# Two norms at a block boundary merged, and the first norm's sums moved into the time of the modulation weights

## The reference, cut to what matters

```
def rmsnorm(x, g):
    return x * rsqrt(mean(x*x) + 1e-6) * g

# first block, layer l
mod = cond @ ada_w[l] + ada_b[l];  sh1, sc1, g1, sh2, sc2, g2 = split(mod, 6)
h = rmsnorm(x, norm1_g[l]) * (1 + sc1) + sh1
x = x + g1 * mixer(h);  x = x + g2 * swiglu(rmsnorm(x, norm2_g[l]) * (1 + sc2) + sh2)
...
x = rmsnorm(x, final_g)                       # end of the first block
# second block, layer 0
h  = rmsnorm(x,   g_mix[0]) * (1 + ca)   + sa
hc = rmsnorm(ctx, g_mix[0]) * (1 + ca_c) + sa_c
q, k, v, u = split(h @ w_in[0]) ...
```

## Time and profile before

| | |
|---|---|
| time, median of 3 runs | 3628.51 us (3627.23 to 3632.27) |
| time of the profiled execution | 3632.27 us |
| span of the profiled execution, first to last instruction | 3631.0 us |
| PE busy | 3426.8 us (94%) |
| POOL, DVE, ACT busy | 1579.2, 1337.1, 794.5 us |
| mean DMA rate | 96 GB/s |
| mean granted TensorE clock | 0.980 |

### The profile page before, as it was taken

How to read it: one execution, slowest core, us unless ns; L and a number is a source line. 1 busy time by engine, 2 the same in 40 slices (tenths; PEclk the granted TensorE clock), 3 DMA queues, 4 the chain that set the end, 5 groups by cost and what they waited for, 6 DMA issues and landing times.

```text
span 3631.0 us, 42550 instructions
## 1 busy us (share of the span) xinstructions
PE 3426.8 (94%) x17456; PEld 2690.6 (74%) x17456; DVE 1337.1 (37%) x2287; ACT 794.5 (22%) x1603; POOL 1579.2 (43%) x996
## 2 busy tenths in 40 slices
PE   5999999999999999999999699889999989889998
PEld 3767777788876677777778577778888878667886
DVE  5853313311158433132111665651211255551113
ACT  2234411100022444111000334320100123420111
POOL 2423266566644133664665331234333333235664
PEclk9999999999999999999999899999999999999999
DMA  6344123333233341335443211122433311114221
GB/s 204 109 134 139 46 81 107 112 95 93 81 99 122 121 136 47 93 99 161 126 140 91 71 36 36 35 80 75 149 109 107 108 53 58 35 47 137 95 93 58
DMA packets 403370, 346.80 MB, mean 96 GB/s; under 512 B 9701, under 2 KB 400613, under 8 KB 403178
## 3 DMA queue, kind: packets, MB, share of 16 engines
q1 hardware_dynamic: 395328, 336.62, 29.7%
q10 hardware_dynamic: 7850, 7.47, 0.7%
HBM read 341.96 MB, written 2.10 MB: 95 GB/s over the span
## 4 chain that ended last, share of the span: by engine, by line
PE 88%; DVE 6%; ACT 3%; DMA 1%; issue 1%; POOL 1%; ACTq 0%; DVEq 0%; SPq 0%; POOLq 0%
PE psum L571 25%; PE psum L572 24%; PE psum L573 24%; PE psum L553 2%; PE psum L812 2%; PE psum L927 1%; PE psum L956 1%; DVE psum L1782 1%; PE psum L800 1%; PE psum L744 1%; PE psum L640 1%; PE psum L787 1%; DVE k L2261 1%; DMA raw_weights<-in_ada_w 1%; PE psum L785 1%
## 5 line engine op out<-in xcount | busy, mean ns | idle before, releaser
L513 POOL TENSOR_SCALAR weights_hi<-raw_weights 128x1024 fp32r<-128x1024 f32 (+3 forms) x496 | 500.3, 1009 | 1980.9 <-PE psum L573 1667.0
L571 PE MATMUL psum<-h_hi,weights_hi 128*128 128x512 f32 (+1 forms) x2832 | 1143.4, 404 | 69.6 <-DVE h_lo L1806 51.4
L516 POOL TENSOR_TENSOR weights_lo<-raw_weights,weights_hi 128x1024 fp32r<-128x1024 f32 (+3 forms) x496 | 1088.0, 2194 | 41.4
L572 PE MATMUL psum<-h_lo,weights_hi 128*128 128x512 f32 (+1 forms) x2832 | 1077.8, 381 | 0.0
L573 PE MATMUL psum<-h_hi,weights_lo 128*128 128x512 f32 (+1 forms) x2832 | 1077.0, 380 | 0.0
L571 PEld LDWEIGHTS psum<-h_hi,weights_hi 128*128 128x128 f32 x2832 | 540.5, 191 | 229.9 <-issue 108.7
L572 PEld LDWEIGHTS psum<-h_lo,weights_hi 128*128 128x128 f32 x2832 | 541.2, 191 | 115.7 <-issue 15.9
L573 PEld LDWEIGHTS psum<-h_hi,weights_lo 128*128 128x128 f32 x2832 | 539.1, 190 | 110.5
L571 PE MATMUL psum<-hidden_hi,weights_hi 128*128 128x512 f32 (+1 forms) x1120 | 413.8, 369 | 0.0
L572 PE MATMUL psum<-hidden_lo,weights_hi 128*128 128x512 f32 (+1 forms) x1120 | 413.7, 369 | 0.0
L573 PE MATMUL psum<-hidden_hi,weights_lo 128*128 128x512 f32 (+1 forms) x1120 | 413.1, 369 | 0.0
(11 more groups left out here) (264 smaller groups left out, 3616.3 us busy)
## 6 DMA issues: line engine op xcount, KB each, us to landing
raw_weights<-in_ada_w SPq DMA_DIRECT2D x96, 1024.0 KB, 5.3
raw_weights<-in_w_mlp SPq DMA_DIRECT2D x64, 1024.0 KB, 5.2
raw_weights<-in_w_in SPq DMA_DIRECT2D x54, 1024.0 KB, 5.4
raw_weights<-in_w_ffn_in SPq DMA_DIRECT2D x88, 512.0 KB, 5.2
raw_weights<-in_w_out SPq DMA_DIRECT2D x16, 1024.0 KB, 4.9
raw_weights<-in_w_ffn_out SPq DMA_DIRECT2D x16, 1024.0 KB, 5.0
raw_weights<-in_w_in SPq DMA_DIRECT2D x30, 512.0 KB, 4.6
raw_weights<-in_w_branch SPq DMA_DIRECT2D x56, 128.0 KB, 2.2
```

The source lines that it names most:

```text
L513: gpsimd.tensor_scalar(whi[:, r, c0:c1], raw[:, raw_slot, c0:c1], 1.0, 1.0, ALU.mult, ALU.mult).then_inc(*split_hi.up(*key, half))
L516: gpsimd.tensor_tensor(wlo[:, r, c0:c1], raw[:, raw_slot, c0:c1], whi[:, r, c0:c1].bitcast(F32), ALU.subtract).then_inc(*split.up(*key, half))
L571: tensor.matmul(out, sh, mh, start=first, stop=False, skip_group_check=shared)
L572: tensor.matmul(out, sh, ml, start=False, stop=False, skip_group_check=shared)
```

## The change

Two places are rewritten.

**Start.** The raw buffers are no longer zeroed and SP issues its first three slabs at once. ACT issues the layer's columns ahead of x, then does the sines, the squares of x and the root, and only then the copy of the "start" row. DVE does the sines' product, query bias, the additions of squares and the reciprocal before ada_finish("start"). PE makes the sums of norm1 after seven of the eight slabs of "start". The group "norm1" of layer 0 is empty: its two slabs go to the end of "rope", in the order behind the slab of B's values.

**Boundary.** final1 and in1 are merged for the 512 tokens. Behind each residual slice ACT makes two squares, of x and of x * final_g, and DVE two additions. PE sums both. ACT and DVE compute the joint factor through logarithms: log1 = Ln(mean1 + eps), inverse1 = Exp(-log1), mean2 * inverse1 on DVE, Ln(... + eps), + log1 on DVE, Exp(-0.5 ...). The column of the scale takes final_g in (scales_g1). X itself is scaled behind in1, by leave(), with Exp(-0.5 log1). The context's squares, sum, root and reciprocal, the lambdas and the columns of in1 move into the last feed-forward of the first block; the context's two matmuls stand between its last up projection and its last down projection. norm_g1, lambda_columns and layer_columns_2 get places of their own in SBUF for that.

```diff
-        g["norm1", l] = slots(l, 8, 10)
-        g["rope", l] = slots(l, 10, 14)
+        g["norm1", l] = slots(l, 8, 10 if l else 8)
+        g["rope", l] = slots(l, 10 if l else 8, 14)
...
         part("B", "v", 0)
+        ada_some("rope", 4, 6)
...
+    gf1 = top.take("norm_g1", [P, KT])
+    lams = top.take("lambda_columns", [P, 8])
+    pcol2 = top.take("layer_columns_2", [P, 2 * KT + 4 + 1])
...
-    work2 = Map(nc, ffn2.at).take("squares_2", [P, 3, TA])
+    sums2 = Map(nc, ffn2.at)
+    work2 = sums2.take("squares_2", [P, 3, TA])
+    roots = sums2.take("roots", [P, 2, T])
+    log1, inverse1 = roots[:, 0, :], roots[:, 1, :]
...
-            if n < RAW:
-                sync.wait_ge(*dve_misc.at("raw", r))
-            elif order[n - RAW][0][0] == "ada":
+            if n >= RAW and order[n - RAW][0][0] == "ada":
                 sync.wait_ge(*ada_row.at(*order[n - RAW][0]))
-            else:
+            elif n >= RAW:
...
-        def norm(segs, work, which, l):
+        def sums(segs, work, which, l):
...
+        def norm(segs, work, which, l):
+            if (which, l) != ("norm1", 0):
+                sums(segs, work, which, l)
...
+        def sum_of(which, l, s, n, bk, work, x0, x1):
+            tensor.wait_ge(*free[bk])
+            tensor.wait_ge(*paired.at(which, l, s, KT - 2))
+            tensor.matmul(bank[bk][:, 0:n], meanm, part_of(work, 0, x0, x1), start=True, stop=False)
+            tensor.wait_ge(*squared.at(which, l, s, KT - 1))
+            tensor.matmul(bank[bk][:, 0:n], meanm, part_of(work, 1, x0, x1), start=False,
+                          stop=True).then_inc(*meaned.up(which, l, s))
+
+        def enter(segs):
+            sum_of("final1", None, 0, T, 2, work1, TC, TA)
+            sum_of("in1", 0, 0, T, 7, work2, TC, TA)
+            free[6] = h_lo.at("in1", 0, 1, KT - 1)
+            for k in range(KT):
+                pending[k] = [h_lo.at("in1", 0, s, k) for s in range(2)]
+            free[4], free[5] = h_lo.at("in1", 0, 0, KT - 1), h_lo.at("in1", 0, 1, KT - 1)
+            free[2], free[7] = dve_misc.at("log12"), dve_misc.at("tokens", KT - 1)
...
+                if l == DEPTH - 1 and t0 == CHUNKS1[-1][0]:
+                    sum_of("ctx1", 0, 0, TC, 6, work2, 0, TC)
...
-            norm([(TC, TA, TC, 1), (0, TC, 0, 2)], work2, "in1", L)
+            both = [(TC, TA, TC, 1), (0, TC, 0, 2)]
+            if L:
+                norm(both, work2, "in1", L)
+            else:
+                enter(both)
...
-        finish(ada_steps("start"))
+        start = ada_steps("start")
+        for _ in range(ROUND - 1):
+            next(start)
+        sums([(TC, TA, 0, 0)], work1, "norm1", 0)
+        finish(start)
         for l in range(DEPTH):
             first_layer(l)
-        norm([(TC, TA, 0, 0)], work1, "final1", None)
...
+        layer_columns(0)
         scalar.dma_start(X[:, :, TC:TA], a["x_t"].rearrange("(k p) t -> p k t", p=P)).then_inc(*loaded["x"].up())
...
+                scale = gf1[:, k:k + 1] if (which, l, s) == ("in1", 0, 0) else 1.0
                 scalar.activation(part_of(work, 1 + (k + 1) % 2 if k else 0, x0, x1), X[:, k, x0:x1],
-                                  ACT.Square).then_inc(*squared.up(which, l, s, k))
+                                  ACT.Square, scale=scale).then_inc(*squared.up(which, l, s, k))
...
+        def enter_root():
+            scalar.wait_ge(*meaned.at("final1", None, 0))
+            scalar.activation(log1, bank[2][:, :], ACT.Ln, bias=eps[:, 0:1]).then_inc(*act_misc.up("log1"))
+            scalar.wait_ge(*act_misc.at("log1"))
+            scalar.activation(inverse1, log1, ACT.Exp, scale=-1.0).then_inc(*act_misc.up("inverse1"))
+            scalar.wait_ge(*dve_misc.at("mean2"))
+            scalar.activation(bank[7][:, :], bank[7][:, :], ACT.Ln, bias=eps[:, 0:1]).then_inc(*act_misc.up("log2"))
+            scalar.wait_ge(*dve_misc.at("log12"))
+            scalar.activation(bank[7][:, :], bank[7][:, :], ACT.Exp, scale=-0.5).then_inc(*rooted.up("in1", 0, 0))
+
         def norm(segs, which, l, hi):
-            root(segs, which, l)
+            if (which, l) == ("in1", 0):
+                enter_root()
+            elif (which, l) != ("norm1", 0):
+                root(segs, which, l)
...
+                if l == DEPTH - 1 and t0 == CHUNKS1[1][0]:
+                    lambdas(0)
+                    scalar.wait_ge(*loaded["g1"].at())
+                    for n in range(KT):
+                        square(n, [(0, TC, 0, 2)], work2, "ctx1", 0, [loaded["ctx"].at()])
...
+                layer_columns2(0)
             feed(l)
+            if l == DEPTH - 1:
+                scalar.wait_ge(*meaned.at("ctx1", 0, 0))
+                scalar.activation(bank[6][:, 0:TC], bank[6][:, 0:TC], ACT.Sqrt,
+                                  bias=eps[:, 0:1]).then_inc(*rooted.up("in1", 0, 1))
...
                 square(n, seg, work1, *key, [summed.at(l, "down", CHUNKS1[-1][0], n, 0)])
-
-        def layer_columns(l):
-            scalar.dma_start(pcol[:], a["cols1"][l]).then_inc(*loaded["cols"].up(l))
+                if l == DEPTH - 1:
+                    square(n, seg, work2, "in1", 0, [summed.at(l, "down", CHUNKS1[-1][0], n, 0)])
...
+            if L == 0:
+                scalar.wait_ge(*scaled.at("in1", 0, 0, KT - 1))
+                scalar.activation(bank[7][:, :], log1, ACT.Exp, scale=-0.5).then_inc(*act_misc.up("rstd1"))
...
         scalar.wait_ge(*loaded["cond"].at())
         scalar.activation(cond_sigmoid[:], cond_in[:], ACT.Sigmoid).then_inc(*act_misc.up("cond"))
-        finish(ada_steps("start"))
         scalar.wait_ge(*dve_misc.at("angles"))
         scalar.activation(ropec[:], ropec[:], ACT.Sin)
         scalar.activation(ropes[:], ropes[:], ACT.Sin).then_inc(*act_misc.up("sines"))
-        layer_columns(0)
         for n in range(KT):
             square(n, [(TC, TA, 0, 0)], work1, "norm1", 0, [loaded["x"].at()])
+        root([(TC, TA, 0, 0)], "norm1", 0)
+        finish(ada_steps("start"))
         scalar.dma_start(gf1[:], a["final1_cols"]).then_inc(*loaded["g1"].up())
         for l in range(DEPTH):
             first_layer(l)
-        root([(TC, TA, 0, 0)], "final1", None)
-        scalar.wait_ge(*loaded["ctx"].at())
-        for n in range(KT):
-            square(n, [(TC, TA, TC, 1), (0, TC, 0, 2)], work2, "in1", 0, [summed.at("final1", n), loaded["ctx"].at()])
         for dst, name in ((cos2, "cos2"), (sin2, "sin2"), (perm2, "perm2"), (edge, "edge")):
             scalar.dma_start(dst[:], a[name]).then_inc(*loaded["axial"].up())
         scalar.dma_start(gf2[:], a["g_final_cols"]).then_inc(*loaded["g2"].up())
-        layer_columns2(0)
-        lambdas(0)
...
-        for r in range(RAW):
-            vector.memset(raw[:, r, :], 0.0).then_inc(*dve_misc.up("raw", r))
...
+        def enter():
+            vector.wait_ge(*meaned.at("in1", 0, 0))
+            vector.wait_ge(*act_misc.at("inverse1"))
+            vector.tensor_tensor(bank[7][:, :], bank[7][:, :], inverse1, ALU.mult).then_inc(*dve_misc.up("mean2"))
+            vector.wait_ge(*act_misc.at("log2"))
+            vector.tensor_tensor(bank[7][:, :], bank[7][:, :], log1, ALU.add).then_inc(*dve_misc.up("log12"))
+            vector.wait_ge(*rooted.at("in1", 0, 0))
+
+        def leave():
+            vector.wait_ge(*act_misc.at("rstd1"))
+            for k in range(KT):
+                vector.scalar_tensor_tensor(out=X[:, k, TC:TA], in0=X[:, k, TC:TA], scalar=gf1[:, k:k + 1],
+                                            in1=bank[7][:, :], op0=ALU.mult,
+                                            op1=ALU.mult).then_inc(*dve_misc.up("tokens", k))
...
-                then = None
+                    lambdas(0)
+                    second_scales(0)
+                    then = [([(0, TC, 0, 2)], work2, "ctx1", 0)]
                 if t0 == CHUNKS1[-1][0]:
-                    then = (work1, "norm1", l + 1) if l < DEPTH - 1 else (work1, "final1", None)
+                    seg = [(TC, TA, 0, 0)]
                     if l < DEPTH - 1:
+                        then = [(seg, work1, "norm1", l + 1)]
                         first_scales(l + 1)
+                    else:
+                        then = [(seg, work1, "final1", None), (seg, work2, "in1", 0)]
+                        vector.wait_ge(*rooted.at("in1", 0, 1))
+                        vector.reciprocal(bank[6][:, 0:TC], bank[6][:, 0:TC]).then_inc(*inverted.up("in1", 0, 1))
+                        vector.wait_ge(*inverted.at("in1", 0, 1))
                 residual(("down", t0), l, 5, [(TC, TA, 0, 0)], then)
...
+            if L == 0:
+                vector.wait_ge(*dve_misc.at("scales", "in1", 0, 2))
+                vector.wait_ge(*loaded["g1"].at())
+                vector.tensor_tensor(col[:, 0, :, 1], col[:, 0, :, 1], gf1[:], ALU.mult).then_inc(*dve_misc.up("scales_g1"))
...
             norm(both, "in1", L, gh, gl)
+            if L == 0:
+                leave()
...
         angles()
```

(17 more changed lines are left out.)

49 lines of the change are left out of this document (30 added, 19 removed).

## The result

| | before | after |
|---|---|---|
| time, median of 4 runs each on one chip | 3629.45 us | 3587.32 us (3585.99 to 3587.93) |
| ratio, with its 95% interval | | 0.9883 [0.9872, 0.9895] |
| span of the profiled execution | 3631.0 us | 3585.5 us |
| mean granted TensorE clock | 0.980 | 0.982 |

The change saves 42.1 us, 1.2%. The profiled executions are 45.5 apart, because the one of before, 3632.27, was above its median.

What follows compares the result with a forecast made beforehand. TensorE, busy in 94% of the span, was taken as the bound, so only its idle holes pay: 20.0 - 2.0 + 18.9 - 1.0 = 35.9 us saved, 3592.6 against the median of 3628.5, range 3584 to 3603.

Steps and rivals of the forecast that it cites:

- Start: Before the first projection matmul: it moves from 65.86 to 45.9, gaining 20.0 us, bounds 16.5 and 21.
- rival (b): At the start, three early slabs starve the small constants: start gains 14, total 30, 3598.6 us; chance 0.12.
- Two slabs in top: Two moved ada slabs now cost TensorE time in top of the first layer: 2.0 us, bounds 2 and 5.
- Boundary: Between first and second block: the hole before the second block's first matmul closes by 18.9 us, bounds 15 and 21.5.
- ACT has five transfers to issue first, so about 2.4: At the boundary, before the chain of logarithms: five transfer issues, 0.46 us apart, occupy ACT until 2025.1.
- Rival (a): At the boundary, one table set serves Ln and Exp: factor ready 2.4 us earlier, 3590; chance 0.08.
- leave(): Ahead of rope2: eight scalings, 5.36 us, and a 0.7 wait fit DVE's 6.77 idle; costs nothing, uncovered up to 6.
- the context's sums: Last feed-forward of the first block: the context's two matmuls now stand in TensorE's busy stretch, costing about 1.0 us.
- Rival (c): Boundary gap closes by only 13 us, through leave(), DVE additions beside POOL or a late table transfer; 3598.5; chance 0.13.
- rival (d): TensorE's granted clock falls elsewhere: 0.970 costs 35 us and takes all, 0.968 gives about 3635; chance 0.02.
- (e): At the start, squares wait so long that TensorE takes its eighth slab after 50: start gains 9, 3604; chance 0.02.
- This stays in both versions: After each hole TensorE runs 5 to 6 us at granted clock 0.50; remaining holes of 10 us or more keep this.

Runs made afterwards that it cites:

- early-sums run: Changed kernel with the sums of norm1 after six of the eight "start" slabs instead of seven; 3582.89 us, ratio 0.9874.
- the two halves: Two runs: the changed kernel with its boundary undone, 3610.83 us, ratio 0.9957; the changed kernel with its start undone, 3604.45 us, ratio 0.9939.

## Why the prediction held, and where it was off

Against the two profiled executions the sum misses 9.6: 45.5 measured, 35.9 forecast. Against the medians, 42.1, it misses 6.2. Term by term:

**Start, 20.0 forecast, 19.4 measured: right, with two errors that cancel in part.** The seventh slab was taken 1.5 earlier than before (32.81 for 34.33), where 2.0 were put in. The loads started at 0.73, but rival (b)'s mechanism happened as well: with slabs in flight from the first, cond came 2.3 later. It cost nothing in the end, since the eight slabs and not cond set the end of this stage; the rival's price rested on 4 us and on the squares, and the squares had slack. The sums took 2.8 instead of 3.75, as the second pair ran at full pace (1.02 for two matmuls), and the reciprocal was done at 41.60 instead of 42.2. What was too low by more was the column operations: I took 0.9 for a POOL operation beside them "up to 2.4" long, and the row is 1.77. The early-sums run shows the same operation at 0.17 where it ran ahead of POOL's.

**Two slabs in top, 2.0 forecast, 2.7 measured**, inside the bounds of 2 and 5.

**Boundary, 18.9 forecast, 20.2 measured from the last residual slice, which itself came 0.45 late (0.3 of it forecast).** The step that was off is "ACT has five transfers to issue first, so about 2.4". The issues start at 2001.90 on ACT's queue, beside the two squares of the last slice and not behind them; of them only 1.14 of idle time is left before the first table load. The logarithm thus begins 4.45 behind the last residual slice, where the forecast had 5.7. The rest of the chain went as written: four loads, and from the start of Ln to the first scaling 6.54, forecast 6.6. Rival (a) is out: each of Ln, Exp, Ln, Exp had its load, in line with the earlier trace rows, and the Trainium skill, page "ScalarE: Activation LUTs", section "Table sets: the hidden batching unit", by which one load serves both functions, is contradicted by the measurement in this program. By the Trainium skill, section "What ACT_TABLE_LOAD costs" of the same page, a switch is a load of about 1.28 and a drain, 2.66 in all. The load's 1.28 is what the trace has; the drain is not seen, since the activation starts 0.01 behind the load and the load 0.02 behind the activation ahead of it.

**Behind it.** leave() cost nothing, with 0.89 left of the cover that I put at 0.7 more than it needs; the context's sums cost 0.95 for 1.0. Rival (c) thus failed by less than 1 us. The granted clock is 0.982, so rival (d) is out; (e) is out, the eighth slab is multiplied at 37.4.

**The clock behind the holes.** "This stays in both versions" was not quite so. Behind the boundary's hole PE ran at 0.50 up to 2019.5, 3.9 us, where it was 5.3 before; at the start it was 3.5 (46.48 to 50.0) for 5.0. The hole in front of the first matmul was 6.86 long there, and not "10 us or more". These 1.4 and 1.5 at half pace give back some 0.7 each, an estimate.

**What the sum lacked: the places.** I read in the diff that three small tiles get places of their own, and gave that no term. It moved everything behind them. In after this was worth about 5: h2's 256-column matmuls became some 3.5 ns slower (116.1 to 119.7 ns between direct neighbours at full clock) and took back, some 4 us, what hidden2 gained in layer 0, so that layer's net is near 0, and the last layer gained 5.4. 5.4 of places and 1.3 of issues, less 0.6, 0.7 and 0.4 of the small terms, are 5.0 above the forecast; the 4.3 of the second layer make 9.3 of the 9.6 of the profiles. That the places did this in hidden2 is shown by moving hidden2 alone; that h2 did the opposite is read from the paces. The 4.3 had no term either. They go with the new start in the traces of before, after and the two halves, and their cause is open. The range held by luck, because the start and the boundary had bounds wide enough for something else: none of my cases contained this term, and places elsewhere could have cost or given far more than the range allowed, as the 41 us of the kernel with all tiles at 128 show.

## What to carry to other kernels

When an edit adds or moves a tile in SBUF, write down the byte of every tile behind it, and ask of each whether its matmuls could change pace; compare the start-to-start time of equal matmuls in stretches that the edit does not touch, before the gain is put down to the edit. In a kernel bound by TensorE such a comparison is worth making for its own sake: here a placement gave more than rewriting two norms. And when holes are priced, issues of transfers on an engine's queue run beside its other work, while a small operation of VectorE can grow to the length of what GpSimd runs beside it: here one of 8 columns took 1.77 beside POOL and 0.17 without, though three others at 41.63, which read PSUM, took 0.34 together beside the same POOL operation.

## What the runs showed of the hardware that was not expected

- The pace of the projections' 512-column matmuls at full granted clock depends on where both the activations' tile and the weights' tile lie modulo 256 bytes: 227 to 229 ns with both at 128, 232.4 with the activations at 128 and the weights at 0, 233.3 at the places of before. On this kernel that is 41 us (from after) and 49.9 us (from before). The 256-column matmuls do not follow it: those of h2 took 116.1 ns at 64, 119.1 at 0, 119.4 at 128 and 119.7 at 224, with the weights at 128, and 119.0 at 128 with the weights at 0. Both equal to some other value than 128 was not run, nor were weights_hi and weights_lo moved apart, nor is it known whether the weight load or the stream of activations is what slows down.
- A kernel whose two profiles show a hole 2.8 us shorter had, measured twice, the median of the kernel with the longer hole. A profile is one execution; a gain of 0.1% read from it need not be in the median.
- A small load shared the DMA engines with three 1 MB slabs issued at 0.73: the cast behind it waited 4.70 and ran at 9.55, while before, with slabs issued from 3.02, it ran at 7.28, right behind DVE's zeroing, and the same chain let PE start 2.3 earlier.
